# Three routers of a two-block network: half of the norm moved to ScalarE and GpSimd, small VectorE work and column sums moved

## The chip, the cores and the metric

One core of one Trainium2 chip runs one kernel. The metric is device time in microseconds (us) for one execution. TensorE has two clock levels, 1.2 and 2.4 GHz; the profile shows the granted one as a share of full speed.

## The reference

Two blocks work on 256 tokens of width 1024 in float32. Three of their parts are mixtures of experts, called e1, e2 and e3 below. Each has a router in front. Cut to what matters here:

```
first block:  x = x + mixer(x)                      # attention and state space model
              x = x + moe(rmsnorm(x, norm_ffn_g))   # e1: 32 experts of 1024 x 256
second block, twice (e2, e3):
              x = layer_norm(ALPHA*x + y @ w_o, ln1_g, ln1_b)
              x = layer_norm(ALPHA*x + moe(x), ln2_g, ln2_b)    # 32 experts of 1024 x 512
moe(t):  g_logits = t @ w_rg + b_rg;  g = argmax;  g_w = softmax(g_logits)[g]
         top 2 of the 8 expert logits of group g; weights softmax(top_v) * g_w
         out = sum over the chosen experts of weight * (silu(t@w_gate) * (t@w_up)) @ w_down
```

## The kernel before

The engines are programmed one by one, each in written order; semaphores join them. A list of milestones per engine says in which order it tells what it has done (`finish(eng, who, name)`), and `after(eng, who, name)` waits for one.

**Weights.** All expert weights pass from HBM through a ring of 12 half slots of 1 MB in on-chip memory, with two more half slots beside it. SyncE issues the loads in written order. Before each it waits until TensorE has used the half slot (`used[...]`). e1 takes 12 MB per step in 8 steps, e2 and e3 take 12 MB per step in 16 steps. A router is followed by step 0 of its experts. While a router runs, SyncE can fill the ring with step 0 and part of step 1 and no more, since nothing is released until step 0 has used its gate weights.

**Router**, written as `moe(e)` on each engine, and before it `residual_rms` (e1) or `residual_norm` (e2, e3):

1. The residual sum of tokens 0 to 127 (th 0) and then of tokens 128 to 255 (th 1) is made on VectorE (L1961). TensorE transposes the raw sums (L826) and makes the 36 router logits per token from them (L955). The norm's scale is applied to the logits afterwards (L2077), so the logits do not wait for the normed tokens. For this the router weights of e2 and e3 are scaled by the norm's gain and centred, which needs column sums of the weights (L980, `column_sums`), made by TensorE within the router of the layer before.
2. VectorE also norms the tokens themselves, in place in `x_sb` for e2 and e3 (L1978 `centred`: (x - mean) * gain row; L1983 `shifted`: * 1/std + offset row), into `xh` for e1 (L2030). ScalarE supplies the square root (L1806).
3. VectorE then picks group and two experts in a chain of small instructions (L2077 to L2101): each waits for the one before. It ends in `sel`, the one-hot of both experts.
4. TensorE counts and ranks from `sel` (L1002 to L1008), VectorE reads count (L2112) and rank (L2121), and makes the selection matrix S (L2136, L2138).
5. TensorE gathers the tokens of the first experts (L1020) from normed tokens and S. Then the experts' matmuls start (L1113).

Around this TensorE also writes the residual into four PSUM banks (L973, `residual_start`, needs normed tokens) and runs products with zeros (L940, `idle_products`), which change no result. ScalarE copies `x_sb` to bfloat16 (L1589) and makes two exponentials for the experts' weights. GpSimd (Pool) scales the router weights, builds tables for a convolution (L792) and, after `e2_items`, centres the third router's weights (L778 to L780).

Of the kernel before, what the change touches and what calls it, by code (L numbers as in the profile page):

```python
# [28 lines left out]
P = 128  # L29
# [24 lines left out]
KEYS_AT, VALUES_AT = 2, 3  # L54
TAPS = 31
# [43 lines left out]
def _build(ctx, nc, ins, out):  # L99
# [264 lines left out]
    def plan_moe(name):  # L364
        for n in range(4):
            use((name + "xT", n), 2 + n)
        use((name + "logits",), 6)
        if name != "e3":
            use((name + "sums",), 5)
        use((name + "count",), 6)  # L370
        use((name + "rank",), 7)

    plan_moe("e1")
    before_moe = {"e1": list(uses)}
    use(("memk",), 5)
    use(("memv",), 6)
# [134 lines left out]
    def normed(ln, e):  # L511
        return [ln + "_add0", ln + "_add1", ln + "_var0", e + "_tok0", ln + "_add2", ln + "_add3", ln + "_var1", e + "_tok"]
# [3 lines left out]
                "ssm_state1", "qk_ms", "f_abs", "qk_tok", "logf"] + [f"ssm_state{n}" for n in range(2, 2 * NQ)] + ["y_ssm", "x1_0", "x1_1", "x1_ms0", "e1_tok0", "x1_2", "x1_3", "x1_ms1", "e1_tok1a", "e1_tok"] + moe_steps("e1")  # L516
# [3 lines left out]
        "act": ["x_sq0", "x_rms0", "x_sq1", "x_rms1", "ssm_dt", "ssm_mag", "ssm_sin", "qk_rms", "f_ln", "glu_sigmoid", "gate3_sigmoid", "x1_sq0", "x1_rms0", "x1_sq1", "x1_rms1", "e1_ge", "e1_p2", "x2_0", "x2_1"]  # L520
        + [f"conv_gate{n}" for n in range(MT)] + ["conv_std", "ln21_std0", "ln21_std1", "e2_ge", "e2_p2", "e2_hi", "e2_mid0", "e2_mid1", "ln22_std0", "x3_0", "ln22_std1", "x3_1",
                                                  "ln31_std0", "ln31_std1", "e3_ge", "e3_p2", "e3_hi", "e3_mid0", "e3_mid1", "ln32_std0", "ln32_squares1", "ln32_std1"],
        "pool": ["ident", "c_zeros", "masks", "alpha_id", "no_sum", "powers_low", "tap_id", "router1", "router2", "router_done2", "router3", "tap_w", "spans", "router_done3"]}
# [49 lines left out]
    def _(sp):  # L573
# [18 lines left out]
        for part, e in enumerate(("e1", "e2", "e3")):  # L592
# [62 lines left out]
            elif e == "e1":  # L655
                after(sp, "vec", "e1_tok")
# [37 lines left out]
    def _(po):  # L694
# [79 lines left out]
        def centred_router(n):  # L774

            w = routers[n - 1]
            evacuated(po, f"e{n - 1}sums")
# [8 lines left out]

        after(po, "vec", "e1_tap_col")
# [8 lines left out]
        finish(po, "pool", "tap_w")  # L796
        po.wait_ge(flag("moe_sum_ready"), 1)
# [3 lines left out]
        after(po, "vec", "e2_items")  # L801
        centred_router(3)
# [3 lines left out]
    def _(pe):  # L806
# [135 lines left out]
        def moe(e, tok):  # L942
# [33 lines left out]
            def column_sums(c):  # L976

                w = (routers[int(e[1])], wr_shift)[c]
                for k in range(KD):
                    last = mm(psum[:, plan[(e + "sums",)][0], c * NR:(c + 1) * NR], ones[:, :], w[:, k, :],  # L980
                              start=(k == 0), stop=(k == KD - 1))
                return last
# [54 lines left out]
            after(pe, "vec", e + "_split")  # L1037
            moe_wait(pe, e, "S", 1)
            gather(0, 0)
            gather(0, 1)  # L1040
            for b in (5, 6):
                pe.wait_ge(bank_free[b], before_moe[e][b])
# [16 lines left out]
            def step_(u, i, keys=False, values=False):  # L1059
# [1681 lines left out]
```

## Time and profile before

| | us |
|---|---|
| median of 3 timed runs | 1700.19 |
| the three | 1695.7, 1700.19, 1704.02 |
| span of the profiled execution, first to last instruction | 1691.3 |
| TensorE busy in it | 1588.8 |
| VectorE, ScalarE, GpSimd busy | 512.4, 276.6, 35.9 |

No separate time is given for the profiled execution; its span is 4.4 us under the fastest timed run and 8.9 us under the median. The routers stand in it at about 228 to 248 us (e1), 584 to 603 us (e2) and 1203 to 1222 us (e3). A busy TensorE is not TensorE at its peak, since the ends of matmuls are modelled.

### The profile page before, as it was taken

How to read it: one execution, taken by the hardware profiler on the slowest of the kernel's cores; microseconds unless marked ns; L12 is line 12 of the kernel's file. 1: busy time of each engine (PE TensorE's matmuls, PEld its weight loads, DVE VectorE, ACT ScalarE, POOL GpSimd, SP SyncE). 2: the span in 40 equal slices, each digit the busy share in tenths (PEclk: the TensorE clock that was granted, in tenths of full speed). 3: DMA queues.
4: the chain of work that ended last, by engine and by line, in shares of the span. 5: the costliest groups of instructions: out<-in, count | busy, mean ns of one | idle time of the engine just before them, and what ended most of it. 6: DMA issues, size and time to landing. Idle time of an engine off the chain costs nothing.

```text
span 1691.3 us, 30927 instructions
## 1 busy us (share of the span) xinstructions
PE 1588.8 (94%) x12619; PEld 795.8 (47%) x12620; DVE 512.4 (30%) x1162; ACT 276.6 (16%) x549; POOL 35.9 (2%) x78
## 2 busy tenths in 40 slices
PE   7999999876799999999999999999899999999997
PEld 5487765533467544343433333674543434333332
DVE  7994333110157551111111111414631111111113
ACT  2304120000035221000100100213210100010011
POOL 4000000100000000000000000000000000000000
PEclk9999999988899999999999999999999999999999
DMA  6422759999983189999999999831399999999996
GB/s 252 150 100 92 298 222 420 421 420 421 422 342 146 68 340 422 422 422 422 422 422 422 422 422 425 359 143 57 149 388 422 422 422 422 422 422 422 422 422 257
DMA packets 79528, 570.25 MB, mean 337 GB/s; under 512 B 8878, under 2 KB 12390, under 8 KB 14566
## 3 DMA queue, kind: packets, MB, share of 16 engines
q1 hardware_dynamic: 77750, 563.41, 81.2%
q10 hardware_dynamic: 1712, 5.92, 0.9%
q8 instruction: 47, 0.77, 0.2%
q14 instruction: 19, 0.16, 0.0%
HBM read 568.24 MB, written 1.05 MB: 337 GB/s over the span
## 4 chain that ended last, share of the span: by engine, by line
PE 57%; DMA 31%; DVE 8%; issue 2%; ACT 1%; SPq 1%; POOL 0%; DVEq 0%; ACTq 0%; POOLq 0%
DMA space<-in_e_up 30%; PE psum L1113 20%; PE psum L1152 8%; PE psum L901 6%; PE psum L1165 4%; PE psum L838 3%; PE psum L1033 3%; PE psum L846 2%; PE psum L1481 2%; DVE space L2398 1%; PE psum L1441 1%; PE psum L1020 1%; PE psum L879 1%; PE psum L1492 1%; PE psum L1381 1%
## 5 line engine op out<-in xcount | busy, mean ns | idle before, releaser
L1113 PE MATMUL psum<-space 128*32 (+1 forms) x5056 | 521.7, 564 | 54.9 <-DMA space<-in_e_up 49.2
L1113 PEld LDWEIGHTS psum<-space 128*32 128x32 f32 x5056 | 167.3, 113 | 395.3 <-issue 386.4
L1152 PE MATMUL psum<-space 128*32 128x512 f32 (+1 forms) x2304 | 255.5, 594 | 6.6 <-DMA space<-in_e_down 6.5
L2194 DVE TENSOR_TENSOR space<-space,psum 128x512 f32<-128x512 f32 (+1 forms) x40 | 25.4, 634 | 581.4 <-PE psum L1113 581.4
L1165 PE MATMUL psum<-space 128*128 128x512 f32 x320 | 150.3, 612 | 0.0
L1152 PEld LDWEIGHTS psum<-space 128*32 128x32 f32 x2304 | 71.9, 110 | 161.0 <-issue 161.0
L1165 PEld LDWEIGHTS psum<-space 128*128 128x128 f32 x320 | 54.2, 189 | 96.5 <-issue 71.8
L2201 DVE COPY space<-psum 128x512 f32<-128x512 f32 x40 | 27.6, 691 | 230.3 <-PE psum L1152 230.3
L1610 ACT ACTIVATE space<-psum 128x512 f32<-128x512 f32 (+1 forms) x40 | 22.2, 554 | 415.7 <-PE psum L1113 415.7
L1033 PE MATMUL psum<-space,xT 128*128 128x128 bf16 x1024 | 89.4, 219 | 0.0
L838 PE MATMUL psum<-xT,space 128*128 128x256 f32 x384 | 85.2, 381 | 3.0 <-ACT xT L1545 1.0
L1579 ACT ACTIVATE space<-psum 128x512 f32<-128x512 f32 x43 | 25.7, 597 | 356.0 <-PE psum L1033 266.9
L1033 PEld LDWEIGHTS psum<-space,xT 128*128 128x128 bf16 x1024 | 68.0, 98 | 27.2 <-issue 26.8
L838 PEld LDWEIGHTS psum<-xT,space 128*128 128x128 f32 x384 | 72.3, 190 | 14.5 <-issue 5.0
L901 PE MATMUL psum<-xT,space 128*128 128x256 f32 x320 | 74.1, 384 | 0.0
L1033 PE MATMUL psum<-space,PT_buf 128*128 128x128 bf16 x512 | 70.4, 219 | 0.0
L901 PEld LDWEIGHTS psum<-xT,space 128*128 128x128 f32 x320 | 59.1, 190 | 11.5 <-issue 4.1
L2153 DVE COPY space<-psum 128x512 f32<-128x512 f32 x43 | 29.7, 691 | 112.2 <-PE psum L1033 78.4
L1616 ACT ACTIVATE space<-psum 128x512 f32<-128x512 f32 x40 | 23.9, 597 | 232.5 <-PE psum L1152 232.5
L846 PE MATMUL psum<-space,xT 128*128 128x512 f32 (+1 forms) x128 | 49.0, 541 | 0.2 <-PE psum L1268 0.2
L1033 PEld LDWEIGHTS psum<-space,PT_buf 128*128 128x128 bf16 x512 | 39.4, 98 | 0.0
L1020 PE MATMUL psum<-space 128*128 128x128 f32 x288 | 37.5, 286 | 0.0
(405 smaller groups left out, 1392.9 us busy)
## 6 DMA issues: line engine op xcount, KB each, us to landing
space<-in_e_up SPq DMA_DIRECT2D x160, 1024.0 KB, 19.9
space<-in_e_down SPq DMA_DIRECT2D x160, 1024.0 KB, 20.5
space<-in_e_gate SPq DMA_DIRECT2D x156, 1024.0 KB, 20.9
space<-in_stream SPq DMA_DIRECT2D x25, 2048.0 KB, 15.5
rows<-in_rows ACTq DMA_DIRECT2D x9, 512.0 KB, 8.8
rows<-in_e_gate SPq DMA_DIRECT2D x4, 1024.0 KB, 26.3
space<-in_stream SPq DMA_DIRECT2D x3, 1024.0 KB, 9.6
x_sb<-in_x SPq DMA_DIRECT2D x2, 512.0 KB, 4.1
```

Of the source, the lines that this page charges most:

```text
L838: last = mm(psum[:, b, n * T:(n + 1) * T], w[:, k, c * P:(c + 1) * P], rhs[:, k, :], start=(k == 0), stop=(k == K - 1))
L846: last = mm(psum[:, b, 0:c1 - c0], lhs[:, k0 + k, th * P:(th + 1) * P], w[:, k, c0:c1], start=(start and k == 0), stop=(stop and k == K - 1))
L901: last = mm(psum[:, b, n * T:(n + 1) * T], w[:, k, c * P:(c + 1) * P], rhs[:, k, :], start=(k == 0), stop=(k == K - 1))
L1020: last = mm(psum[:, (4, 7)[half], k * P:(k + 1) * P], tok[:, th, (4 * half + k) * P:(4 * half + k + 1) * P], S[:, par, th, :], start=(th = ...
L1033: last = mm(psum[:, (4, 7)[half], k * P:(k + 1) * P], parts[n][th][:, cols], S_half[:, par, th, :], start=(n == 0 and th == 0), stop=(n == ...
L1113: last = mm(psum[r, 5 + g, 0:FW], xg[:, u, k, r], w, start=(k == 0), stop=(k == KD - 1))
L1152: last = mm(psum[r, (4, 7)[half], :], hT[:, f, r], w, start=(f == 0), stop=(f == F - 1))
L1165: last = mm(psum[:, 2 * th + half, :], SwT[:, th * P:(th + 1) * P], og[:, half * 512:(half + 1) * 512], start=False, stop=False, skip_grou ...
L1481: return mm(psum[:, b, :], yT[:, k, th * P:(th + 1) * P], w[:, k % 4, hf * 512:(hf + 1) * 512], start=not started, stop=(k == MT - 1))
L1579: act(xg[:, par, 0:4, :], psum[:, 4, :].rearrange("p (k c) -> p k c", k=4), ACT.Copy).then_inc(flag("moe_xgA"), 1)
L2153: ve.tensor_copy(xg[:, par, 4:8, :], psum[:, 7, :].rearrange("p (k c) -> p k c", k=4)).then_inc(flag("moe_xgB"), 1)
L2201: ve.tensor_copy(og[:, 512:1024], psum[:, 7, :]).then_inc(flag("moe_outB"), 1)
```

## The change

Five things are done in the three routers.

1. The norm of tokens 128 to 255. VectorE now makes only two numbers per token (1/std and -mean/std, told as `ln.._off1`; in e1 only the first, `x1_r1`). ScalarE makes the normed tokens in one instruction of 128x1024 (`.._xhat`), and Pool multiplies with the gain row and, in e2 and e3, adds the offset row (`gained`), each 128x1024. `e?_tok` is now told by Pool. SyncE (e1) and ScalarE's loads of the next norm rows (e2, e3) wait for it there.
2. TensorE's queue. The residual of banks 2 and 3 moves from in front of the count to behind the rank. In front of the count stand 9 products with zeros, in front of the gather 3.
3. VectorE. The clears of two tables move in front of the norm (`clear_tables`). The inputs of both exponentials and, for e2 and e3, the two instructions that store the choice of pairs move behind the first S. The first `gathered` comes before the first `shares_of`.
4. ScalarE copies to bfloat16 before the exponentials.
5. The column sums for routers 2 and 3 leave the routers and go into steps 1 and 5 of e1's experts; Pool centres router 3 in e1 too.

```diff
+SUMS_AT = {1: 2, 5: 3}
@@ Pool
+        def gained(e, dst, *rows_):
+            after(po, "act", e + "_xhat")
+            for row, op in zip(rows_, (ALU.mult, ALU.add)):
+                step(po.tensor_tensor(dst, dst, row, op))
+            finish(po, "pool", e + "_tok")
+        gained("e1", xh[:, 1, :], gain)
...
+        for e in ("e2", "e3"):
+            gained(e, x_sb[:, 1, :], rows[:, 0, :], rows[:, 1, :])
@@ TensorE, moe
             for b in range(2):
                 residual_start(b)
-            if e != "e3":
-                after(pe, "pool", f"router{int(e[1]) + 1}")
-                open_bank(pe, e + "sums")
-                column_sums(0)
-            if e != "e1":
-                after(pe, "vec", e + "_tok")
-            for b in range(2, 4):
-                residual_start(b)
-            if e == "e3":
-                idle_products(0, 5)
+            idle_products(0, 9)
...
-            if e != "e3":
-                close_bank(column_sums(1), e + "sums")
-            idle_products(1, {"e1": 0, "e2": 3, "e3": 7}[e])
+            after(pe, "pool", e + "_tok")
+            for b in range(2, 4):
+                residual_start(b)
+            idle_products(2, 3)
@@ ScalarE, moe
+            if e != "e1":
+                full(ac, e + "logits")
+                step(act(parts[0][0], x_sb[:, 0, :], ACT.Copy))
+                after(ac, "pool", e + "_tok")
+                step(act(parts[0][1], x_sb[:, 1, :], ACT.Copy))
+                finish(ac, "act", e + "_hi")
@@ ScalarE, layer_norm
+                    after(ac, "vec", name + "_off1")
+                    step(act(x_sb[:, 1, :], x_sb[:, 1, :], ACT.Identity, bias=ln_off[:, 1:2], scale=ln_r[:, 1:2]))
+                    finish(ac, "act", e + "_xhat")
-        after(ac, "vec", "e2_tok")
+        after(ac, "pool", "e2_tok")
         load_rows(3)
@@ VectorE, residual_norm, th 1
-                    for cols in halves:
-                        centred(a, th, cols)
                     scaled(ln, a, th)
-                    for cols in halves:
-                        shifted(th, cols)
-                tell(e + ("_tok0", "_tok")[th])
+                    step(ts(ln_off[:, 1:2], bn2[:, 1, 0:1], ln_r[:, 1:2], -1.0, ALU.mult, ALU.mult))
+                    tell(ln + "_off1")
```

VectorE in e3, from the last statistics of the norm (BN_AGGR) to the choice of the group, before: `x_sb` holds the tokens, `rows` the gain and offset rows.

```order
L1966 BN_AGGR small<-small 128x2 [waits vec_chain]
L1967 TENSOR_SCALAR small<-small 128x1 [waits vec_chain]
L1978 SCALAR_TENSOR_TENSOR x_sb<-x_sb,small,rows 128x512 [waits vec_chain,bank_full5,bank_full4]
L1978 SCALAR_TENSOR_TENSOR x_sb<-x_sb,small,rows 128x512 [waits vec_chain]
L1973 RECIPROCAL small<-small 128x1 [waits act_finished,vec_chain]
L1983 SCALAR_TENSOR_TENSOR x_sb<-x_sb,small,rows 128x512 [waits vec_chain] x2
L2624 MEMSET small 128x1 [waits vec_chain]
L2077 SCALAR_TENSOR_TENSOR space<-psum,small,r_bias 128x36 [waits bank_full6,pool_finished,constants_loaded,vec_chain]
```

And the same place in the changed kernel:

```order
L1984 BN_AGGR small<-small 128x2 [waits vec_chain]
L1985 TENSOR_SCALAR small<-small 128x1 [waits vec_chain]
L1991 RECIPROCAL small<-small 128x1 [waits vec_chain,act_finished]
L2029 TENSOR_SCALAR small<-small 128x1 [waits vec_chain]
L2099 SCALAR_TENSOR_TENSOR space<-psum,small,r_bias 128x36 [waits vec_chain,pool_finished,bank_full6,constants_loaded]
L2099 SCALAR_TENSOR_TENSOR space<-psum,small,r_bias 128x36
L2105 TENSOR_REDUCE space<-space 128x2 [waits vec_chain,bank_free6]
```

Four instructions of 128x512 are gone between the statistics and the logits; one of one column per partition is new.

TensorE in e2 between the logits and the gather, before (`alpha_id` marks the residual's products, `ones` with 36 columns the column sums):

```order
L973 MATMUL psum<-x_sb,alpha_id 128x512 [waits bank_free0,vec_finished,pool_finished]
L973 MATMUL psum<-x_sb,alpha_id 128x512 [waits bank_free1]
L980 MATMUL psum<-wr,ones 128x36 [waits bank_free5,pool_finished]
L980 MATMUL psum<-wr,ones 128x36 x7
L973 MATMUL psum<-x_sb,alpha_id 128x512 [waits bank_free2,vec_finished]
L973 MATMUL psum<-x_sb,alpha_id 128x512 [waits bank_free3]
L1002 MATMUL psum<-space,ones 128x32 [waits vec_finished,bank_free6]
L1003 MATMUL psum<-space,ones 128x32
```

And now:

```order
L983 MATMUL psum<-x_sb,alpha_id 128x512 [waits bank_free0,vec_finished,pool_finished]
L983 MATMUL psum<-x_sb,alpha_id 128x512 [waits bank_free1]
L950 MATMUL psum<-no_sum 128x512 [waits pool_finished]
L950 MATMUL psum<-no_sum 128x512 x8
L1004 MATMUL psum<-space,ones 128x32 [waits vec_finished,bank_free6]
L1005 MATMUL psum<-space,ones 128x32
```

The second half of the residual and 8 column-sum products no longer stand in front of the count; nine products with zeros do.

GpSimd from step 5 of e1's experts to the router of e2, changed kernel (`wr` holds the router weights of e3):

```order
L801 TENSOR_TENSOR space<-tap_id,tap_col 128x1024 [waits pool_made] x3
L779 TENSOR_SCALAR wr_sums<-wr_sums 128x36 [waits pool_made,bank_free5]
L780 TENSOR_TENSOR wr<-wr,wr_sums 128x288 [waits pool_made]
L781 TENSOR_TENSOR r_bias<-wr_sums,brow 128x36 [waits pool_made]
L809 MEMSET space 128x16x30 [waits pool_made,moe_sum_ready]
L809 MEMSET space 128x16x4 [waits pool_made]
L792 TENSOR_TENSOR x_sb<-x_sb,rows 128x1024 [waits pool_made,act_finished]
L792 TENSOR_TENSOR x_sb<-x_sb,rows 128x1024 [waits pool_made]
```

The last two rows are new, come again for e3, and with one operation (`gain`) for e1; the centring (L779 to L781) stood behind L809 before.

## Rows read from the trace of the kernel before

**Rows 1.** The page, parts 4 (chain) and 6 (DMA issues).

```profile
PE 57%; DMA 31%; DVE 8%; issue 2%; ACT 1%; SPq 1%; POOL 0%; DVEq 0%; ACTq 0%; POOLq 0%
...
space<-in_e_up SPq DMA_DIRECT2D x160, 1024.0 KB, 19.9
```

**Rows 2.** Windows at routers e1, e2, e3: length, busy times, clock, DMA share, GB/s.

```profile
230.00:256.00 26.00, 26.00 (x246) 19.88 (x245) 11.24 (x45) 5.32 (x11) 0.00 (x0) 0.87 1.02 395
603.50:608.00 4.50, 4.50 (x48) 1.30 (x40) 4.22 (x9) 0.55 (x1) 0.00 (x0) 1.00 0.19 33
1218.00:1227.00 9.00, 8.95 (x84) 5.27 (x88) 7.43 (x19) 1.24 (x2) 0.00 (x0) 1.00 0.10 19
```

**Rows 3.** Timeline of VectorE, router e3: start us, length us, instruction.

```profile
1204.82 0.15 DVE L1967 TENSOR_SCALAR small<-small 128x1 f32<-128x1 f32 x1
...
1206.98 1.54 DVE L1983 SCALAR_TENSOR_TENSOR x_sb<-x_sb,small,rows 128x512 f32<-128x512 f32 x2
...
1208.86 0.42 DVE L2077 SCALAR_TENSOR_TENSOR space<-psum,small,r_bias 128x36 f32<-128x36 f32 x2
...
1210.03 0.17 DVE L2089 SCALAR_TENSOR_TENSOR space<-space 128x8 f32<-128x8 f32 x1
...
1213.15 0.23 DVE L2101 TENSOR_TENSOR space<-space 128x64 f32<-128x64 f32 x1
...
1214.65 0.19 DVE L2112 COPY space<-psum 128x32 f32<-128x32 f32 x1
...
1215.98 0.23 DVE L2121 TENSOR_TENSOR space<-psum,space 128x64 f32<-128x64 f32 x1
```

**Rows 4.** Timeline of TensorE, router e3, idle before in brackets.

```profile
1204.31 3.21 PE L955 MATMUL psum<-wr,xT 128*128 128x36 f32 x28
1207.36 3.68 PE L973 MATMUL psum<-x_sb,alpha_id 128*128 128x512 f32 x8
1210.88 1.24 PE L940 MATMUL psum<-no_sum 128*128 128x512 bf16 x5
1213.58 0.38 PE L1002 MATMUL psum<-space,ones 128*128 128x32 f32 x2 [1.46 <-DVEq L530]
...
1218.05 3.81 PE L1020 MATMUL psum<-space,x_sb 128*128 128x128 f32 x32 [1.69 <-DVE space L2138]
```

**Rows 5.** Timeline of ScalarE, router e3.

```profile
1205.06 0.20 ACT L1806 ACTIVATE small<-small 128x1 f32<-128x1 f32 x1
...
1214.43 2.14 ACT L1589 ACTIVATE xT<-x_sb 128x1024 bf16<-128x1024 f32 x2
```

**Rows 6.** Timeline of TensorE, router e2.

```profile
585.06 3.21 PE L955 MATMUL psum<-first_layer,xT 128*128 128x36 f32 x28
588.11 3.66 PE L973 MATMUL psum<-x_sb,alpha_id 128*128 128x512 f32 x4
...
595.11 0.30 PE L1002 MATMUL psum<-space,ones 128*128 128x32 f32 x2
```

**Rows 7.** Timeline of VectorE, router e2.

```profile
589.51 0.42 DVE L2077 SCALAR_TENSOR_TENSOR space<-psum,small,r_bias 128x36 f32<-128x36 f32 x2 [0.24 <-DVE x_sb L1983]
...
597.07 0.22 DVE L2121 TENSOR_TENSOR space<-psum,space 128x64 f32<-128x64 f32 x1
```

**Rows 8.** Timeline of GpSimd and VectorE in e1's experts.

```profile
328.08 8.00 POOL L792 TENSOR_TENSOR space<-tap_id,tap_col 128x1024 f32<-128x1024 f32 x4 [50.10 <-PE psum L1055]
...
274.51 0.43 DVE L2132 TENSOR_TENSOR space<-col_id,space 128x256 f32<-128x256 f32 x1
...
328.64 1.63 DVE L2132 TENSOR_TENSOR space<-col_id,space 128x256 f32<-128x256 f32 x1
```

**Rows 9.** One line of GpSimd (L753): shortest, median, longest in ns, forms.

```profile
L753 POOL TENSOR_TENSOR space<-space x4: 226/300/455, 19.0 to 26.0; 128x16 f32<-128x16 f32 x1, 128x32 f32<-128x32 f32 x1, 128x64 f32<-128x64 f32 x1, 128x128 f32<-128x128 f32 x1
```

**Rows 10.** Timeline of TensorE in e1's step 1, and a window behind it.

```profile
273.70 5.35 PE L1113 MATMUL psum<-space 128*32 128x256 f32 x64 [3.21 <-DMA space<-in_e_up]
...
274.00:277.00 3.00, 3.00 (x36) 1.87 (x32) 1.18 (x4) 0.00 (x0) 2.15 (x4) 0.53 1.03 429
```

More of the change, by code:

```diff
@@ L655, in _ @@
             elif e == "e1":
-                after(sp, "vec", "e1_tok")
+                after(sp, "pool", "e1_tok")
                 load_expert(0, ROWS_SLOT, 1)
@@ L974, in residual_start, with column_sums @@
                    start=True, stop=False, skip_group_check=True)
[L976 to L982, printed above, removed]
+            def column_sums(n):
+                after(pe, "pool", f"router{n}")
+                b = open_bank(pe, f"sums{n}")
+                for c, w in enumerate((routers[n - 1], wr_shift)):
+                    for k in range(KD):
+                        last = mm(psum[:, b, c * NR:(c + 1) * NR], ones[:, :], w[:, k, :], start=(k == 0), stop=(k == KD - 1))
+                close_bank(last, f"sums{n}")
             after(pe, "pool", "alpha_id")
@@ L1040, in moe @@
             gather(0, 1)
+            after(pe, "vec", e + "_split")
             for b in (5, 6):
@@ L1083, in step_ @@
                     memory_values()
+                if sums:
+                    column_sums(sums)
                 moe_wait(pe, e, "xgA", c(1))
@@ L1089, in step_ @@
                         evacuated(pe, "memk")
+                    if sums and g == 0:
+                        evacuated(pe, f"sums{sums}")
                     if values and g == 1:
@@ L1586, in moe @@
             finish(ac, "act", e + "_p2")
-            if e != "e1":
-                for th in range(TH):
-                    step(act(parts[0][th], x_sb[:, th, :], ACT.Copy))
-                finish(ac, "act", e + "_hi")
-            if e != "e3":
-                src = full(ac, e + "sums")
-                copy_out((e + "sums",), wr_sums[:, :], src[:, 0:2 * NR])
             moe_wait(ac, e, "gathA", 1)
@@ L1619, in moe @@
                 for n in range(STEPS[e]):
+                    if n in SUMS_AT:
+                        if SUMS_AT[n] > 2:
+                            after(ac, "pool", f"router_done{SUMS_AT[n] - 1}")
+                        src = full(ac, f"sums{SUMS_AT[n]}")
+                        copy_out((f"sums{SUMS_AT[n]}",), wr_sums[:, :], src[:, 0:2 * NR])
                     if n == KEYS_AT:
@@ L1749, in _ @@
                 take_T("e1xT", (0, 1))
+        after(ac, "vec", "x1_r1")
+        step(act(xh[:, 1, :], x_sb[:, 1, :], ACT.Copy, scale=rms_r[:, 1:2]))
+        finish(ac, "act", "e1_xhat")
         moe("e1")
@@ L1843, in _ @@
         layer_norm("ln31", "e3")
-        after(ac, "vec", "e3_tok")
+        after(ac, "pool", "e3_tok")
         load_rows(7)
@@ L1998, in residual_norm @@
                         stats(n)
+                    clear_tables()
                 variance(ln, th)
-                for hf in range(2):
-                    full(ve, e + "xT", 2 * th + hf)
                 if th == 0:
+                    for hf in range(2):
+                        full(ve, e + "xT", hf)
                     ve.wait_ge(flag(f"rows{a}"), 32)
@@ L2060, in split_pairs, with clear_tables @@
             ve.wait_ge(chain, n)
-            step(ve.tensor_copy(split[:, 0, :], r_choice))
+        def clear_tables():
+            counted(ve.memset(wcomb, 0.0))
+            step(ve.memset(rank, -1.0))
         def moe(e):
@@ L2102, in moe @@
             tell(e + "_sel")
-            step(tt(r_gd, r_L[:, :, 0:NG], over(r_gmax, P, TH, NG), ALU.subtract))
-            tell(e + "_gd")
-            step(tt(r_d21, r_m2, r_m1, ALU.subtract))
-            tell(e + "_d21")
-            counted(ve.memset(wcomb, 0.0))
-            step(ve.memset(rank, -1.0))
             step(ts(r_pen2, sel, -1.0, 1000.0, ALU.add, ALU.mult))
@@ L2155, in moe @@
             places(0, 0, narrow=False)
+            step(tt(r_gd, r_L[:, :, 0:NG], over(r_gmax, P, TH, NG), ALU.subtract))
+            tell(e + "_gd")
+            step(tt(r_d21, r_m2, r_m1, ALU.subtract))
+            tell(e + "_d21")
+            if e != "e1":
+                step(ts(r_choice, r_big, -float(SLOT), float(SLOT), ALU.mult, ALU.add))
+                step(ve.tensor_copy(split[:, 0, :], r_choice))
+            tell(e + "_split")
             after(ve, "act", e + "_ge")
```

43 lines of the change are left out of this document (22 added, 21 removed).

## The prediction

> **What bounds the kernel now.** First the chain of waits on the page: 57% of the span is TensorE, 31% DMA, and VectorE has 8% [rows 1]. The experts are paced by their weights and by TensorE. A router counts only where it delays the weights, so the second view is the DMA share around each router [rows 2]. In e1 the DMA engines are busy without a gap from 230 to 256 us (share 1.02): the loads for steps 0 and 1 are still moving when the experts start. A faster router e1 gains nothing; a slower one costs nothing until this queue has drained. In e2 the ring is full at 603.5 us and the share falls to 0.19 for 4.5 us, that is 3.6 us of idle. In e3 it is 0.10 over 9 us, 8.1 us of idle. These gaps end when step 0 uses its first gate weights, which follows the gather. So a microsecond in routers e2 or e3 is a microsecond of the whole, up to 3.6 us of gain in e2 and 8.1 in e3, without limit for a loss.
>
> Third, the path through router e3, on each engine's timeline. VectorE has the variance at 1204.97, norms until 1208.52, and takes the logits at 1208.86 [rows 3]; TensorE had them at 1207.52 [rows 4]. The choice runs from 1208.86 to 1213.38 (4.52 us), the count is read at 1214.65, the rank at 1215.98, and the gather starts at 1218.05 [rows 3, 4]. In e2 the logits end at 588.27, are taken at 589.51, the choice ends by the same 4.52 us at 594.03, but the count starts only at 595.11, since residual and column sums stand in front of it [rows 6]. The rank is read at 597.07 [rows 7], the gather some 2.07 us behind, as in e3: 599.15.
>
> **Part by part.**
>
> *VectorE's norm.* Its four instructions go. VectorE then waits for TensorE. A product of TensorE reaches a waiting VectorE in some 0.12 us, an estimate. e3: taken at 1207.64 for 1208.86, -1.22 us. e2: 588.39 for 589.51, -1.12.
>
> *Behind the one-hot.* TensorE's count starts 0.20 us after the choice (1213.58 for 1213.38). Two count matmul pairs, 0.22 us apart and 0.39 long, and 0.11 to VectorE give the count at +0.92, against +1.27 before in e3 and +1.8 in e2 (count from 595.11). Behind it two small instructions of 0.2 us (the stored choice and its cast) leave the way to the rank. So I put the rank's reading at +1.95 for +2.60 in e3 (-0.65) and +3.04 in e2 (-1.1). TensorE must then write two residual products (1.84, half of 3.68) and three zeros (0.25 each by 1.24 for 5) behind its rank at +1.5: free at +4.1, just when S is ready (+1.95 and 2.07) [rows 3, 4]. This costs 0 to 0.1 us. The exponentials' inputs move behind S and lie beside the gather's 3.81 us.
>
> *ScalarE and Pool.* From the variance on: ScalarE's root 1205.06 to 1205.26 [rows 5], two VectorE instructions of 0.2 us, 0.23 us to ScalarE, 1.07 us for 128x1024 (half of 2.14 [rows 5]): 1207.0. Pool starts at 1207.2. Pool's price: 4 instructions of 128x1024 took 8.00 us, 2.00 each [rows 8], but two inputs of those are repeated patterns. With whole inputs 16 elements took 226 ns and 128 took 455 [rows 9], 2.04 ns an element, 2.3 us for 1024. Bounds 1.94 and 2.3; I take 2.25, nearer the row with the same kind of inputs. Pool is then busy from 1207.2 to 1211.8 in e3. The logits end 2.55 us behind the variance there; with the same spacing in e2 (logits' end 588.27 [rows 6]) Pool is busy from 587.95 to 592.5. The tokens are there long before the gather.
>
> *What Pool does to VectorE.* This is the price that the diff doesn't show. While Pool worked on L792 from 328.08, VectorE's 128x256 instruction took 1.63 us, where it takes 0.43 at 274.51 [rows 8]: it was held until Pool's first instruction had ended, near 329.85. The chain of the choice is made of such instructions with two inputs in on-chip memory. In e3 the first (equality) is due at 1208.4, held to 1209.4, one or two pass between Pool's instructions, and the one-hot of the group, before at 1210.03 [rows 3], is held to 1211.75: +1.72, with the bound of the scan held too +1.9. By Pool's 1.94 it is +1.1. So the choice ends near 1215.2 instead of 1213.38. Sum e3: +1.8 - 0.65 = +1.15 (+0.45 with the short Pool). Sum e2 likewise: +1.82 - 1.1 = +0.75 (+0.1). Together +1.9, or +0.55 at the low bound; I take +1.5.
>
> The Trainium skill, "SBUF — State Buffer", section "Who interferes with whom", calls the pair of ports shared by the two engines an exclusive lock held for a whole instruction; this row agrees. The skill's page "GPSIMD Engine Reference", section 3.1, gives 4497 ns for a tensor_tensor of 2048 float32; half of it, 2.25 us, would be an estimate for one of these, and the sum by it would be the same +1.9.
>
> *Column sums in e1.* 32 matmul records of 36 columns, 3.7 us by 28 in 3.21 [rows 4], and 0.6 us for ScalarE's copy, in steps 1 and 5. TensorE sat idle 3.21 us in step 1 waiting for weights [rows 10], so about 1 us is not covered there. It is hidden by the queue: a load of 1 MB lands 19.9 us after its issue [rows 1] where 1 MB at 395 GB/s [rows 2] needs 2.7, so a late release by 1 us, even by 4, leaves the DMA engines work. Cost 0. If this cover were gone, see the third rival.
>
> *At nothing, together:* the clears in front of the norm (0.2 us; VectorE waits there for TensorE or the rows' load); ScalarE's order (its copies are needed only by the second gather); SyncE's wait in e1 for Pool (some 2 us later, with a DMA share of 1.02 over it [rows 2]); the next norm rows issued 3 us later, into a queue that is busy or idle for 8 us afterwards; router 3's centring.
>
> **Total.** Against the profiled span 1691.3 + 1.5 = 1692.8 us. The median stands 8.9 us above this span, so 1700.2 + 1.5, forecast **1702 us**. The measurement: three runs spread by 8 us, so 0.5% (8.5 us) is about what can be told from no change.
>
> **The rivals.**
>
> 1. *The hold is not effective* (Pool's real instructions are short, or VectorE passes between them). For it: 0.17 us instructions need little of the port. Against: 1.63 us at 328.64. Then e3: -1.22 - 0.65 = -1.9. e2: choice at 592.9, but TensorE has its cold residual (3.66 us from 588.11 [rows 6]) and nine zeros (2.2) until 594.0, count 1.1 us earlier, rank -1.3. Together -3.2: 1697. Chance 0.24.
> 2. *The clock falls while TensorE waits for the held choice.* In e3 TensorE is idle from 1211.4 (1207.36 + 1.84 + 2.2) to 1215.4, 4 us; before it was 1.46 us [rows 4], and the clock was full. After 3.21 us of idle the granted clock was 0.53, the lower level, for 3 us [rows 10]. Residual and gather would run in it: 3.66 us for 1.84 as in e2 [rows 6], so about +1.7 us per fall, once or in both routers, partly again in the gather. 1700.2 + 1.9 + 1.7 to 3.4, about 1705. Against: the wait in e2 is only 2 us. Chance 0.24.
> 3. *The column sums push e1 (slower than before).* If the loads are not as deep in queue as landing times say, both insertions count in full, 2 x 4.3 = 8.6 us: 1709, over the bound. It decides where the work queued at DMA is below 4.3 us at a release; by the rows it is 17. Chance 0.05.
> 4. *The change does not reach the path at all:* routers within 0.3 us of before, 1700; contained in the forecast's bounds.
>
> **How the numbers follow.** Forecast (0 to +3) 0.42, rivals 0.24, 0.24, 0.05, and 0.05 for what I have not seen, of either sign. Range: from rival 1 less half the runs' spread (1697 - 4) to rival 2 with both falls and the spread (1705 + 4): 1693 to 1709. Faster by over 0.5% would need 8.5 us, more than all terms of gain: 0.05. Slower by over 0.5%: the third rival and some of the unseen, with a little of the second: 0.08. The rest, 0.87, is within 0.5%.
>
> **What would show it.** Right: VectorE's first logits instruction 0.1 us behind TensorE's last logit in e2 and e3; Pool with two instructions of about 2.2 us each; inside them VectorE instructions of 8 or 64 columns that last 1 to 2 us instead of 0.2; the gather at +1.2 us in e3 and +0.8 in e2 counted from the logits' end (10.53 us and 10.88 before); DMA idle a little longer than 8.1 and 3.6 us; e1 unchanged. Wrong: no such long instructions, a gather more than 1 us earlier, a step of e1 over 30 us, or a wait of the gather for Pool.

## The result, and the profile after

| | us |
|---|---|
| before, median of 20 timed runs | 1695.58 (1693.29 to 1704.02) |
| changed, median of 20 timed runs | 1700.12 (1697.92 to 1704.84) |
| ratio | 1.0025, 95% interval 1.0016 to 1.0033: slower by 4.3 us (2.7 to 5.6); the medians differ by 4.5 |
| profiled execution, changed: its time and its span | 1701.91, 1700.2 |

The change costs 4.3 us and is within 0.5%. The forecast was 1702 us and +1.5. Two errors cancel in the first number: the three runs of before that it was made from had a median 4.6 us above that of twenty, and the change was sized 2.8 us too small. That 1702 lies so near 1700 is luck.

One execution is one draw. The profile of before was a lucky one: its span of 1691.3 and the 1.7 us that lie around a span in the changed kernel give 1693.0, 2.6 us under the median. That of the changed kernel is 1.8 us over its median. So the two profiles differ by 8.9 us where the kernels differ by 4.3. Of the 8.9, routers e2 and e3 have 6.5 (logits' end to the gather, below). Another 1.7 lie ahead of e2, in 128 matmuls of the convolution that the change does not touch (before, then changed):

```profile
542.81 7.11 PE L1381 MATMUL psum<-space 128*32 128x256 f32 x128 [1.96 <-DVE space L2555]
543.08 8.80 PE L1388 MATMUL psum<-space 128*32 128x256 f32 x128 [1.97 <-DVE space L2577]
```

From 545 to 547 us the granted clock was 1.00 in the first and 0.52 in the second. All 14 profiles of this case show one of these two lengths, seven each. Call the residual of banks 0 and 1, ahead of the count, the first, and that of banks 2 and 3 the second. Where the convolution's row is 7.11 us, the first residual of e2 then runs in the lower clock (3.44 to 3.66 us for four products); where it is 8.80, that residual runs at full clock (1.96). norm_vec and small_back, whose code differs only in VectorE's order in the routers, fell one on each side. So a profile has its fall of the clock at one place or the other by chance, as far as one profile per kernel can tell, and this matters for what follows. Lengths in one profile are trusted below more than sums over it.

VectorE in router e2, timeline of the changed kernel (the answer to [rows 7]; e3 has the same lengths):

```profile
590.34 0.42 DVE L2099 SCALAR_TENSOR_TENSOR space<-psum,small,r_bias 128x36 f32<-128x36 f32 x2 [1.88 <-PE psum L965]
590.91 0.16 DVE L2105 TENSOR_REDUCE space<-space 128x2 f32<-128x8 f32 x1 [0.15 <-DVEq L2102]
591.11 1.18 DVE L2109 TENSOR_TENSOR space<-space 128x8 f32<-128x8 f32 x1
592.32 0.17 DVE L2110 TENSOR_TENSOR_SCAN space<-group_in,space 128x8 f32<-128x8 f32 x1
592.53 2.19 DVE L2111 SCALAR_TENSOR_TENSOR space<-space 128x8 f32<-128x8 f32 x1
...
597.68 0.23 DVE L2123 TENSOR_TENSOR space<-space 128x64 f32<-128x64 f32 x1
...
600.54 0.23 DVE L2135 TENSOR_TENSOR space<-psum,space 128x64 f32<-128x64 f32 x1 [0.38 <-PE psum L1010]
```

GpSimd there, and ScalarE:

```profile
589.92 4.78 POOL L792 TENSOR_TENSOR x_sb<-x_sb,rows 128x1024 f32<-128x1024 f32 x2 [117.20 <-ACTq L531]
...
592.34 2.36 POOL L792 TENSOR_TENSOR x_sb<-x_sb,rows 128x1024 f32<-128x1024 f32 x1
```

```profile
588.55 1.24 ACT L1826 ACTIVATE x_sb<-x_sb,small 128x1024 f32<-128x1024 f32 x1 [0.58 <-DVEq L531]
```

Pool works from 589.92 to 594.70, in two instructions of 2.35 us with a gap of 0.08 us between them; the second row above is the second of them alone. The equality over 8 columns (L2109) took 0.17 us before:

```profile
590.27 0.17 DVE L2087 TENSOR_TENSOR space<-space 128x8 f32<-128x8 f32 x1
```

Now it lasts 1.18 and ends at 592.29, with Pool's first instruction; the one-hot of the group (L2111) lasts 2.19 and ends at 594.72, with the second. Such a stretched VectorE instruction is called held below. All behind it is as short as ever. The choice ends 7.68 us behind the logits' end, for 5.76.

TensorE there, and in e3 (answers to [rows 6] and [rows 4]):

```profile
587.02 3.21 PE L965 MATMUL psum<-first_layer,xT 128*128 128x36 f32 x28
590.06 1.96 PE L983 MATMUL psum<-x_sb,alpha_id 128*128 128x512 f32 x4
592.08 1.89 PE L950 MATMUL psum<-no_sum 128*128 128x512 bf16 x8
598.11 0.61 PE L1004 MATMUL psum<-space,ones 128*128 128x32 f32 x2 [4.14 <-DVEq L531]
...
600.24 3.76 PE L983 MATMUL psum<-x_sb,alpha_id 128*128 128x512 f32 x4
603.79 1.39 PE L950 MATMUL psum<-no_sum 128*128 128x512 bf16 x3
605.01 3.73 PE L1023 MATMUL psum<-space,x_sb 128*128 128x128 f32 x32
```

```profile
1221.64 0.38 PE L1004 MATMUL psum<-space,ones 128*128 128x32 f32 x2 [4.14 <-DVEq L531]
...
1222.74 3.66 PE L983 MATMUL psum<-x_sb,alpha_id 128*128 128x512 f32 x4
1226.24 0.81 PE L950 MATMUL psum<-no_sum 128*128 128x512 bf16 x3
```

TensorE waits 4.14 us for the choice in both routers. The four products of the second residual then take 3.76 and 3.66 us, nearly twice the 1.96 of 590.06. Windows over these stretches (columns as in [rows 2]) show why:

```profile
600.00:604.00 4.00, 4.00 (x8) 1.70 (x8) 2.94 (x14) 0.41 (x2) 0.00 (x0) 0.50 0.93 377
1218.00:1222.00 4.00, 0.36 (x4) 0.39 (x4) 3.22 (x14) 2.69 (x3) 0.23 (x1) 1.00 0.97 395
1222.00:1226.00 4.00, 4.00 (x13) 2.05 (x13) 3.04 (x14) 1.12 (x3) 0.00 (x0) 0.59 0.40 160
```

The granted clock is 0.50 in e2's residual, the lower level (1.2 GHz); the pairs of count and rank are slow there already, 0.61 us for 0.39. In e3 the clock is full over the wait and falls right behind it. From the logits' end the gather starts at +14.78 us in e2 and +13.13 in e3, for 10.88 and 10.53. The weights pay for it: the DMA engines now idle 7.6 us behind e2 (share 0.16 over 9 us) and 9.0 behind e3 (0.10 over 10 us), where the share is down to 0.40 in the 4 us before that as well. In the kernel before they idled 3.6 us behind e2 and 8.1 behind e3 [rows 2].

```profile
606.00:615.00 9.00, 9.00 (x85) 4.53 (x87) 5.82 (x11) 1.22 (x2) 0.00 (x0) 1.00 0.16 34
1226.00:1236.00 10.00, 10.00 (x88) 5.64 (x90) 6.88 (x20) 0.60 (x1) 0.00 (x0) 0.99 0.10 13
```

### The profile page after: what moved, and what is told of

The parts are those of the page before. It is cut to its first block, busy times and chain, and to the rows that moved or that the text cites. A ratio compares the mean times of both kernels' runs of the same rounds, so it can differ in the third digit from the quotient of the medians.

```text
span 1700.2 us, 30972 instructions
## 1 busy us (share of the span) xinstructions
PE 1596.1 (94%) x12636; PEld 799.8 (47%) x12641; DVE 511.9 (30%) x1154; ACT 280.4 (16%) x552; POOL 46.9 (3%) x83
## 4 chain that ended last, share of the span: by engine, by line
PE 58%; DMA 30%; DVE 8%; issue 2%; ACT 1%; SPq 1%; POOL 0%; DVEq 0%; ACTq 0%; POOLq 0%
DMA space<-in_e_up 24%; PE psum L1120 19%; PE psum L1159 9%; DMA space<-in_e_down 6%; PE psum L911 6%; PE psum L1172 4%; PE psum L848 4%; PE psum L1036 3%; PE psum L856 2%; DVE space L2419 1%; PE psum L1488 1%; PE psum L1448 1%; PE psum L1023 1%; PE psum L1388 1%; PE psum L889 1%
```

## The experiments

Two effects are to be told apart: Pool's hold on VectorE's choice, and the fall of TensorE's clock in the wait that the hold opens. All ratios are to the kernel before, on the same chip. "Gather" is the time from the logits' end to the gather's start in the profiled execution, one per run.

| run | ratio (95%) | gather e2, e3, us | wait before the count e2, e3, us |
|---|---|---|---|
| before | 1 | 10.88, 10.53 | 0, 1.46 |
| changed | 1.0025 (1.0016 to 1.0033) | 14.78, 13.13 | 4.14, 4.14 |
| norm_vec | 0.9974 (0.9963 to 0.9985) | 9.17, 10.67 | 0, 1.72 |
| more_zeros | 1.0014 (1.0002 to 1.0026) | 11.61, 11.61 | 0.27, 0.26 |
| pool_busy | 1.0027 (1.0014 to 1.0040) | 14.60, 10.88 | 4.00, 0.70 |
| sums_only | 1.0002 (0.9992 to 1.0013) | 10.45, 10.54 | 2.45, 1.47 |
| no_zeros | 1.0001 (0.9990 to 1.0011) | 10.71, 12.35 | 1.96, 3.66 |
| norm_vec_z15 | 0.9981 (0.9971 to 0.9992) | 9.11, 11.22 | 0, 0 |
| small_back | 0.9979 (0.9967 to 0.9992) | 9.53, 10.41 | 1.71, 1.72 |
| pool_e1_only | 0.9974 (0.9963 to 0.9986) | 9.01, 9.14 | 0, 0 |
| pool_one | 0.9978 (0.9966 to 0.9990) | 11.00, 9.24 | 2.12, 0.43 |
| pool_pieces | 1.0014 (1.0000 to 1.0028) | 11.42, 14.15 | 2.26, 3.96 |
| resid_front | 1.0019 (1.0006 to 1.0032) | 11.61, 11.59 | 0.84 + 1.32, 0.83 + 1.32 |
| norm_front | 0.9989 (0.9973 to 1.0004) | 9.34, 9.34 | 0, 0 |

The gather's start does not show a fall inside the gather itself. Its 32 matmuls took 3.7 to 4.2 us in all runs but sums_only (5.74 in e2, 5.95 in e3) and resid_front (5.38, 5.17).

**Norm back on VectorE (norm_vec).** The changed kernel, with the norm of tokens 128 to 255 on VectorE; Pool and ScalarE have no part in it.

```diff
@@ VectorE, residual_norm, th 1
-                    step(ts(ln_off[:, 1:2], bn2[:, 1, 0:1], ln_r[:, 1:2], -1.0, ALU.mult, ALU.mult))
-                    tell(ln + "_off1")
+                centred(a, th, whole)
+                scaled(ln, a, th)
+                shifted(th, whole)
+                tell(e + "_tok")
```

> The changed kernel with one part undone: the norm of tokens 128 to 255 is again made by VectorE (two instructions of 128x1024 in e2 and e3, one in e1), all other parts as changed. Theory 1 (Pool's two instructions hold VectorE's choice chain, and the clock of TensorE falls in the wait): no VectorE instruction of the choice is longer than 0.3 us; VectorE takes the logits about 0.65 us behind their end; the gather starts 9.2 us behind the logits' end in e2 and e3 (before 10.88 and 10.53, changed 14.95 and 13.13). Total 3 us under before, 7 us under the changed kernel, clock full in both routers. Rival (the new order of VectorE's and TensorE's small work, or the column sums in e1, cost the time): within 1 us of the changed kernel.

Measured 1692.18 us, ratio 0.9974: 4.4 us under the kernel before, 8.7 under the changed one. All instructions of the choice are 0.16 to 0.29 us long; the two that were held are now, in e2:

```profile
591.51 0.17 DVE L2091 TENSOR_TENSOR space<-space 128x8 f32<-128x8 f32 x1
...
591.92 0.17 DVE L2093 SCALAR_TENSOR_TENSOR space<-space 128x8 f32<-128x8 f32 x1
```

The gather starts at +9.17 us in e2, as expected, but at +10.67 in e3, for 9.2: TensorE waited 1.72 us there, and its second residual took 3.03 us for 1.96. So the clock fell in e3, against the expectation. (For the changed kernel's e2 the expectation says 14.95; the rows give 14.78.) One thing differs from before in the norm itself: this version makes it in two instructions of 128x1024 (1.28 us each) for two pairs of 128x512 (1.54 a pair [rows 3]), so VectorE takes e2's logits 0.73 us behind their end for 1.24. ScalarE's and Pool's part is what costs; the rest of the change, with these whole instructions, gains.

**Pool works on something else (pool_busy).** norm_vec, with two Pool instructions of 128x768 on other data, started behind VectorE's norm.

```diff
+        for e in ("e2", "e3"):
+            gained(e, at(14592, 768), vec[:, 0:768], vec[:, 0:768])
```

> norm_vec with Pool made busy on other data: behind the norm of e2 and e3 it runs a multiplication and an addition of 128x768 on a part of memory that nobody uses, and nobody waits for it. Theory 1: the port is what holds VectorE, whatever the data: two instructions of the choice last up to 1.7 us, the choice ends about 3 us later in each router than in norm_vec, TensorE waits over 4 us and the clock falls: 8 to 11 us over norm_vec. Rival (VectorE was late in the changed kernel because of a dependence on Pool's results or of queue order): no change against norm_vec.

Measured 1.0027, all of the loss. No token waits for Pool here. VectorE in e2:

```profile
592.68 0.97 DVE L2092 TENSOR_TENSOR space<-space 128x8 f32<-128x8 f32 x1
593.68 0.17 DVE L2093 TENSOR_TENSOR_SCAN space<-group_in,space 128x8 f32<-128x8 f32 x1
593.89 1.66 DVE L2094 SCALAR_TENSOR_TENSOR space<-space 128x8 f32<-128x8 f32 x1
```

and Pool:

```profile
591.81 3.71 POOL L792 TENSOR_TENSOR space<-space,vec 128x768 f32<-128x768 f32 x2 [118.13 <-DVEq L531]
```

Pool ends at 595.52 and the one-hot at 595.55. In e3 the same two rows last 1.02 and 1.65 us. The hold follows Pool's own instructions, not the data. The clock fell in e2 (wait 4.00 us, second residual 3.76). In e3 it was low already in the logits (3.85 us for 3.21) and the first residual (3.76), TensorE came late, waited only 0.70 us and kept the full clock behind it: gather at +10.88.

**Pool's second instruction left out (pool_one).** This kernel leaves the addition of the offset row out in e2 and e3, so its tokens are not the reference's.

```diff
-            gained(e, x_sb[:, 1, :], rows[:, 0, :], rows[:, 1, :])
+            gained(e, x_sb[:, 1, :], rows[:, 0, :])
```

> The changed kernel without Pool's second instruction in e2 and e3: the offset row is not added, so Pool works 2.4 us there for 4.8. If VectorE is held for as long as Pool works, the choice ends about 5.7 us behind the logits' end for 7.7 (only the first equality is held, by 1.0 us; the second hold of 2.0 us is gone), TensorE waits 2.1 us for 4.1, and logits' end to gather is 9.8 us at full clock or up to 11.7 where the clock falls, for 14.9 (e2) and 13.1 (e3). The whole is then 4 to 7 us under the changed kernel, ratio to before 0.998 to 1.000. If something else than Pool's work had slowed the choice, the time stays at 1.0025.

Ratio 0.9978, 8 us under the changed kernel, a little more than expected, for 2.4 us less of Pool in each router. The choice is held by Pool's first instruction only and ends 5.66 us behind the logits' end (e2), for 5.76 before: one hold of 1.0 us is what the logits taken 1.1 us earlier give back. The second hold is loss, and it opens the long wait. In e2 the clock fell behind the wait of 2.12 us (residual 2.96 us, gather at +11.00). In e3 the logits and the first residual were slow already (3.54 and 3.35 us), the wait was 0.43 us, and the second residual ran at full clock (1.96, +9.24).

**Pool's instructions in pieces (pool_pieces).**

```diff
-                step(po.tensor_tensor(dst, dst, row, op))
+                for c in range(0, 1024, 256):
+                    step(po.tensor_tensor(dst[:, c:c + 256], dst[:, c:c + 256], row[:, c:c + 256], op))
```

> The changed kernel with each of Pool's 128x1024 instructions cut into four of 128x256, the same work. If the hold is that of a whole Pool instruction (a lock), no VectorE instruction of the choice lasts over some 0.8 us, but more of them are held, since Pool now works about 5.5 us in eight pieces: five to seven instructions at 0.4 to 0.8 us, the choice ends 7 to 8 us behind the logits' end as before the cut, ratio 1.001 to 1.0025. If VectorE and Pool share the memory's port evenly, the long instructions keep their 1.2 and 2.2 us.

VectorE in e2, Pool busy from 589.83 to 596.20 in eight pieces of 0.73 us that start 0.80 us apart:

```profile
591.02 0.36 DVE L2110 TENSOR_TENSOR space<-space 128x8 f32<-128x8 f32 x1
591.41 0.17 DVE L2111 TENSOR_TENSOR_SCAN space<-group_in,space 128x8 f32<-128x8 f32 x1
591.62 0.57 DVE L2112 SCALAR_TENSOR_TENSOR space<-space 128x8 f32<-128x8 f32 x1
592.23 0.17 DVE L2116 TENSOR_SCALAR space<-space 128x8 f32<-128x8 f32 x1
592.43 0.63 DVE L2117 TENSOR_TENSOR space<-space 128x64 f32<-128x64 f32 x1
593.10 0.22 DVE L2119 TENSOR_REDUCE space<-space 128x2 f32<-128x64 f32 x1
593.35 0.52 DVE L2110 TENSOR_TENSOR space<-space 128x64 f32<-128x64 f32 x1
593.90 0.83 DVE L2111 TENSOR_TENSOR_SCAN space<-expert_in,space 128x64 f32<-128x64 f32 x1
594.77 0.70 DVE L2112 SCALAR_TENSOR_TENSOR space<-space 128x64 f32<-128x64 f32 x1
595.51 0.77 DVE L2121 SCALAR_TENSOR_TENSOR space<-space 128x64 f32<-128x64 f32 x1
596.31 0.22 DVE L2122 TENSOR_REDUCE space<-space 128x2 f32<-128x64 f32 x1
```

No held row is over 0.83 us, seven instructions are held for two, and the choice ends where it did, 7.5 us behind the logits' end. A hold ends when Pool's running instruction does: a lock, not a shared rate. Each held row has two inputs in SBUF, the on-chip memory. The reduce at 593.10, with one, passes at its usual length inside a Pool piece (593.06 to 593.78); the tensor_scalar at 592.23 starts in a gap between two pieces and tells nothing. The ratio is 1.0014, inside the expected band.

**More zeros (more_zeros).** The changed kernel with 27 products with zeros for 9 ahead of the count in e2 and e3.

```diff
-            idle_products(0, 9)
+            idle_products(0, {"e1": 9, "e2": 27, "e3": 27}[e])
```

> The changed kernel with 27 instead of 9 products with zeros in front of the count in e2 and e3 (results unchanged), which fill the 4.14 us in which TensorE waits for the choice. Theory 1: the hold stays (VectorE instructions of 1.2 and 2.2 us), the granted clock stays full, and the gather starts 11.7 us behind the logits' end in both routers: 4 to 5 us under the changed kernel in the profile, about 2 us over before. Rival (the clock is not what costs): gather at 13 to 15 us as in the changed kernel, or later because the zeros stand in front of the count.

TensorE in e2:

```profile
598.02 0.38 PE L1004 MATMUL psum<-space,ones 128*128 128x32 f32 x2 [0.27 <-DVEq L531]
...
599.13 1.96 PE L983 MATMUL psum<-x_sb,alpha_id 128*128 128x512 f32 x4
```

The hold is as in the changed kernel (VectorE rows of 1.19 and 2.19 us), TensorE waits 0.27 us, the residual takes 1.96 us and the gather starts at +11.61 in both routers: within 0.1 us of the prediction's own sums at full clock (10.88 + 0.75 and 10.53 + 1.15). The ratio is 1.0014, 1.9 us under the changed kernel.

**The wait alone (no_zeros).** norm_vec without the nine products with zeros in e2 and e3.

> The norm stays on VectorE, as in the run with the norm back, and the nine products with zeros in front of the count of e2 and e3 are left out (e1 keeps them; they change no result). TensorE then waits about 3.7 us for the choice, with no hold on VectorE. If the clock falls in such a wait and this alone is worth what the zeros give back (the clock theory), TensorE's granted clock falls to the lower level ahead of the count in both routers, and logits' end to gather grows from 9.2 us (e2) and 10.7 us (e3) to about 11 in each, and the whole is 2 to 4 us over the run with the norm back (ratio to the kernel before 0.9985 to 1.000). If the wait alone costs nothing and the hold of VectorE was all, it stays within 0.5 us of that run (ratio 0.997).

Ratio 1.0001, 4.5 us over norm_vec and a little over the expected band, with no hold at all. TensorE in e3, and the window over it:

```profile
1212.98 0.54 PE L1001 MATMUL psum<-space,ones 128*128 128x32 f32 x2 [3.66 <-DVEq L531]
...
1215.04 3.76 PE L980 MATMUL psum<-x_sb,alpha_id 128*128 128x512 f32 x4
```

```profile
1213.00:1218.00 5.00, 5.00 (x14) 3.35 (x15) 3.12 (x14) 0.41 (x2) 0.00 (x0) 0.51 0.91 337
```

A wait that costs the path nothing by itself lets the clock fall to 0.51, and residual and zeros (4.84 us from the residual's start to the gather, for 2.61 in norm_vec's e2) then stand between rank and gather. So the fall of the clock costs time by itself. norm_vec's e3 had a fall too (4.10 us from the residual's start to the gather), so the profiles, added over both routers, differ by 3.2 us only.

**Fifteen zeros in e3 (norm_vec_z15).**

```diff
-            idle_products(0, 9)
+            idle_products(0, 15 if e == "e3" else 9)
```

> The norm stays on VectorE; in e3 alone there are 15 products with zeros in front of the count for 9. They fill the 1.72 us that TensorE waited there at a falling clock in the run with the norm back. If the clock follows TensorE's idle time, e3's logits' end to gather falls from 10.67 to about 9.3 us and the whole by 1 to 1.5 us under the run with the norm back, ratio to before about 0.9965. If VectorE's chain alone sets the gather in e3, nothing changes (0.997 to 0.9975).

A miss. In the profiled execution the clock was low already in the logits (3.86 us for 3.21) and the residual (3.76), so that fifteen zeros took 4.39 us and themselves delayed the count. Ratio 0.9981, not separable from 0.9974. Whether fifteen zeros keep the clock up in e3 was thus not seen.

**The residual back in front (resid_front, norm_front).** The changed kernel and norm_vec, with the residual of banks 2 and 3 in front of the count in e2 and e3 (norm_front has 3 zeros there for 9).

```diff
             idle_products(0, 9)
+            if e != "e1":
+                residual_rest()
```

> The changed kernel with one part undone: in e2 and e3 the residual of banks 2 and 3 stands again ahead of the count, behind the nine products with zeros (Pool has the tokens 4.5 us behind the logits' end, 3.2 us before the choice is ready). The hold on VectorE stays. TensorE's wait of 4.1 us is cut in two pieces of 0.5 and about 1.5 us, and nothing but three zeros stands between rank and gather. By the clock theory logits' end to gather falls to 11.6 us in both routers, as with more zeros, and the ratio to before is about 1.001. If the clock falls all the same, S still sets the gather and it is 12 to 12.5 us, ratio 1.0015. If the residual's place did not matter, 1.0025 stays.

> The norm stays on VectorE, as in the run with the norm back, and in e2 and e3 the residual of banks 2 and 3 stands ahead of the count, with three products with zeros there for nine. If the residual's move behind the rank is what this run gained over the kernel before, logits' end to gather grows from 9.2 to 10.5 us in e2 and the ratio returns from 0.997 to 0.9985 or more. If the order of VectorE's small work and the absent column sums gave it, S sets the gather at 9.2 us whatever stands in TensorE's queue and the ratio stays at 0.997.

resid_front: the gather starts at +11.61 and +11.59 as expected, but the ratio is 1.0019, for about 1.001. Two waits of 0.84 and 1.32 us left the clock full; behind a third, 1.80 us between three zeros and the gather, it fell inside the gather itself:

```profile
602.77 5.38 PE L1030 MATMUL psum<-space,x_sb 128*128 128x128 f32 x32 [1.80 <-DVE space L2159]
```

5.38 us for 3.81, and 5.17 in e3: the fall moved one step on. norm_front: S sets the gather at +9.34 in both routers, within 0.2 us of norm_vec in e2, and its gather ran at full clock behind the same 1.80 us of idle. The expectation's two signs disagree: the gather says that S sets it whatever stands in TensorE's queue, the ratio of 0.9989 (0.9973 to 1.0004) says that the residual's place had a part. It cannot be told from norm_vec, nor quite from before, so this stays open.

**The rest of the change (sums_only, small_back, pool_e1_only).** The kernel before with only the column sums moved (`SUMS_AT`); norm_vec with the exponentials' inputs and the clears back behind the one-hot; norm_vec with ScalarE's and Pool's norm in e1 alone.

```diff
@@ small_back, VectorE behind the one-hot
+            step(tt(r_gd, r_L[:, :, 0:NG], over(r_gmax, P, TH, NG), ALU.subtract))
+            tell(e + "_gd")
+            step(tt(r_d21, r_m2, r_m1, ALU.subtract))
+            tell(e + "_d21")
+            clear_tables()
```

> The kernel before with only the column sums moved into steps 1 and 5 of e1's experts, and router 3 centred there. Theory 1: e1's end within 0.5 us of before since its loads are 17 us deep in queue; in e2 the count starts with the choice and the gather 0.5 us earlier: total 0 to 1 us under before. Rival (the sums push e1): 4 to 8 us over before, all of it at e1's end.

> The norm stays on VectorE, and of the changed order on VectorE one part is undone: the inputs of the exponentials and the clears of the tables stand again right behind the one-hot, ahead of the count's reading. If these small instructions lie on the path (as the prediction had it, -0.65 us in e3), count and rank are read 0.35 to 0.65 us later in each of e2 and e3 and the whole is 0.7 to 1.3 us over the run with the norm back. If they are covered by TensorE's count, rank and gather start stay within 0.1 us and the time is the same.

> ScalarE and Pool norm the second half in e1 alone; e2 and e3 keep the norm on VectorE. If e1 is covered by the queue of weight loads (the prediction), the whole is that of the run with the norm back, ratio to before about 0.997, though e1's choice is held by 0.6 us for one Pool instruction. If e1 counts, it is 0.5 to 1 us over that run and e1's step 0 ends later by as much.

sums_only: 1.0002, no difference. The last matmuls of e1's experts start at 467.99 for 467.82, 0.2 us later; that is little beside the 1.6 us by which norm_vec and no_zeros differ there with the same code for e1. The gather starts 0.4 us earlier in e2 (0.5 was expected), but in this profile the clock fell in both gathers (5.74 and 5.95 us). In e3 that is the kernel before's own order with nearly its waits (1.47 and 1.20 us for 1.46 and 1.69), and there it stayed full. small_back: the gather is 0.4 us later in e2, and TensorE waits 0.36 us for S there; 0.8 us in the whole by the ratios, inside their error. pool_e1_only: 0.9974, the same as norm_vec, though TensorE waits 0.26 us for the held choice in e1. Routers e2 and e3 of its profile had their slow stretch in the first residual (3.51 and 3.66 us), where nothing waits for it, and the full clock from the count on: the gather starts at 9.01 and 9.14 us, which is what norm_vec's code gives when no fall comes behind the count.

## Why the prediction was right, and which term was too small

- *E1 hidden, e2 and e3 on the path.* Right: pool_e1_only and sums_only change nothing that their ratios could show.
- *VectorE's norm gone: logits taken 0.12 us behind their end.* Right: 590.23 to 590.34, 0.11 us.
- *Pool's price, 2.25 us each (1.94 to 2.3).* 2.35, just over the upper bound, and 4.78 for both with the gap; ScalarE's 1.24 us for 1.07. It has a part in the 0.1 us by which e2's choice came later than forecast.
- *The hold: +1.8 us to the choice.* Right: +1.92 in e2 and +1.81 in e3, in rows of 1.18 and 2.19 us. Rival 1 is out. This price, which the diff does not show, is real: pool_busy gives the whole loss though VectorE keeps its norm. The Trainium skill, "SBUF — State Buffer", section "Who interferes with whom", says that VectorE instructions with two inputs in SBUF contend with a GpSimd instruction that reads SBUF, and that those with at most one, outside the two-port modes, do not. The traces agree: the held rows of pool_pieces have two such inputs, while a reduce of 0.22 us and, in the changed kernel, the two logits' instructions with one input in PSUM (0.42 us together at 590.34) passed beside Pool at their usual lengths.
- *Behind the one-hot: rank read at +1.95.* Right at full clock: 1.85 in e3, and in pool_one's e2 as well. In the changed kernel's e2 it was 2.63, with count and rank in the lower clock (0.61 us a pair for 0.39).
- *The residual behind the rank: "free at +4.1, just when S is ready", "This costs 0 to 0.1 us".* **This term failed.** From the rank's reading to the gather the prediction had 2.07 us; it was 4.47 (e2) and 3.61 (e3), +2.40 and +1.54. The residual that was moved behind the rank fits beside S only at full clock (1.96 us). After the wait it takes 3.66 to 3.76.
- *The wait before it.* Put at 4 us in e3 (4.14) and only 2 us in e2 (4.14). The 2 us came from before's e2, whose first residual ran in the lower clock (3.66 us [rows 6]); here it ran at full clock, ended earlier, and the wait grew. So the clock fell in both routers. But the slow first residual of before does occur behind the change too: in pool_pieces' e2 (3.47 us) the wait was 2.26 us and the clock stayed full. How often each case comes, one profile per kernel cannot say.
- *Rival 2, the clock.* It, not the forecast, is what the profile shows. The measured change of 4.3 us lies outside the forecast's 0 to +3 and inside rival 2's +3.6 to +5.3 (1.9 + 1.7 to 3.4). The number of the forecast was met by the high median of before alone; from the median of twenty runs, 1695.6, its +1.5 would have given 1697.1, 3.0 us too low.
- *Rivals 3 and 4.* Out: no loss that can be seen from the column sums, and the path did move. (Rival 3's 1709 is 1700.2 + 8.6; with the +1.5 of the other terms it would have been 1710.)

By router: e2 misses 14.78 - 11.63 = 3.15 us, of which 2.40 behind the rank, 0.68 before its reading and 0.10 in the choice; e3 misses 13.13 - 11.68 = 1.45, of which 1.54 behind the rank. That profile was on the slow side; the medians' miss is 2.8 us for both together.

What stays open is how the 8.7 us between changed kernel and norm_vec divide. By profiles, gathers added, the clock is 4.7 us (changed against more_zeros). The hold is 3.4 us against norm_vec, whose e3 had a fall of its own, and 5.1 against pool_e1_only, the same code for e2 and e3 without a fall behind the count. By medians the hold is 6.8 and the clock 1.9, each with some 2.5 to 2.8 us of uncertainty. The lower price of the clock by medians would fit a changed kernel whose clock does not fall in both routers in every execution; this was not shown. Hold and clock are not independent either: no_zeros pays 4.5 us for a wait without hold. Nor was it fully separated what makes norm_vec 4.4 us faster than before: the whole norm instructions give 0.5 us a router by their rows, the small work on VectorE about 0.4 (small_back), and the rest was not tried alone.

## What to carry to other kernels

Work moved to an idle engine is free only if the memory ports that it needs are idle too. Here each short VectorE instruction with two inputs in SBUF that started inside a long Pool instruction was held to its end. So put such Pool work where VectorE waits or reads one input from SBUF; cutting it into pieces did not help a chain (choice 7.5 us behind the logits' end, for 7.7). When a hand-over on TensorE gets later, cost the wait twice: once as time, once as what runs behind it at half the clock. Do not put work that "just fits" at full clock behind such a wait. Leave the norm on VectorE and keep the rest: that version ran 4.4 us under the kernel before.

## What the hardware showed that was not expected

- Similar waits of TensorE had different outcomes. After 1.71 us (small_back, e2) the residual took 1.96 us; after 1.72 us (small_back and norm_vec, e3) 2.77 and 3.03; after 1.80 us the gather took 3.81 us in norm_front and 5.38 in resid_front. After 2.12 us (pool_one, e2) the residual took 2.96, after 2.26 us (pool_pieces, e2) 1.96. After 3.66, 3.96, 4.00 and 4.14 us the lower clock followed every time. So one profile cannot price a wait of about 2 us.
- What TensorE did before the wait sorts most of these. Count the passes of e2 and e3, over all 14 profiles, with a wait of 1.3 us or more ahead of the count or the gather. Where the first residual had run at full clock, the clock fell behind the wait in 12 of 14 (not in small_back's e2 and before's e3). Where that residual had itself been slow, it fell in 1 of 4 (no_zeros' e2, 1.96 us; not in pool_pieces' e2 nor norm_front's two). No run tested this.
- A scan with two inputs (L2110) passed at 0.17 us, in each router, while its neighbours were held. It started at 592.32, in the gap ahead of Pool's second instruction (592.34 to 594.70), and ran to 592.49 beside it. In pool_pieces the scan at 591.41 passed in the same way, but the one at 593.90, 0.04 us behind the start of a Pool piece (593.86), lasted 0.83. So in these rows the one that started first went through.
- Pool's 128x1024 took 2.35 us and its 128x256 0.73, four of which are a quarter longer than the whole (2.90 us), with a gap of 0.08 us behind each besides. VectorE's 128x1024 norm instruction took 1.28 us.
